# A mixture-of-experts encoder on one core: summed rows and the ninth weight unit later, bfloat16 one-hots, the last expert pair's weights in halves

## The reference, cut to what matters

```python
mod = (c_act @ w_mod[l] + b_mod[l])[:, None, :]
sh1, sc1, g1, sh2, sc2, g2 = jnp.split(mod, 6, axis=-1)
...
mix = jnp.concatenate([y_pool, y_gla], axis=-1) @ w_out[l]
x = x + g1 * mix
h = rms_norm(x) * (1.0 + sc2) + sh2
x = x + g2 * moe_ffn(h, w_router, b_router, w1[l], w3[l], w2[l])
...
# in moe_ffn, for a token t of expert e with its weight wt:
hid = jax.nn.silu(x_pad[tok] @ w1[e]) * (x_pad[tok] @ w3[e])
out[tok] += (hid @ w2[e]) * wt
...
return rms_norm(x) * final_g
```

## Time and profile before

| | us |
|---|---|
| median of 3 runs (755.04 to 759.0) | 756.38 |
| the profiled execution | 761.83 |
| its span in the trace | 760.0 |

### The profile page before, as it was taken

One profiled execution on the slowest core, in us unless ns is written; L12 is line 12 of the kernel. 1 busy time (PEld: TensorE's weight loads), 2 busy tenths in 40 slices (PEclk: granted clock), 3 DMA queues, 4 the chain that ended last, 5 costly groups with the idle time before them and its releaser, 6 DMA issues.

```text
span 760.0 us, 9258 instructions
## 1 busy us (share of the span) xinstructions
PE 700.8 (92%) x3822; PEld 388.3 (51%) x3822; DVE 343.1 (45%) x624; ACT 174.9 (23%) x309; POOL 55.5 (7%) x55
## 2 busy tenths in 40 slices
PE   3799999999898799989779999999999999998893
PEld 2578778777687444443424443443443443453442
DVE  3554988698865213323314233333333333332326
ACT  4332376532232020210110101110110110110104
POOL 2007700100000100000000000000000000000000
PEclk9899999999999899999987999999999999999997
DMA  9995353844738389998996999999999999999962
GB/s 337 388 382 202 139 200 132 314 147 206 292 137 347 131 354 427 426 425 326 430 425 281 420 415 427 426 426 426 426 428 427 426 427 428 425 428 427 429 286 110
DMA packets 38922, 259.42 MB, mean 341 GB/s; under 512 B 4126, under 2 KB 4510, under 8 KB 26208
## 3 DMA queue, kind: packets, MB, share of 16 engines
q1 hardware_dynamic: 34416, 250.11, 80.5%
q0 software_dynamic: 2688, 4.88, 1.7%
q10 hardware_dynamic: 1776, 3.84, 1.3%
HBM read 259.20 MB, written 4.19 MB: 347 GB/s over the span
## 4 chain that ended last, share of the span: by engine, by line
PE 75%; DMA 16%; DVE 7%; issue 1%; ACT 1%; SPq 1%; DVEq 0%; POOLq 0%
PE bank L904 26%; PE bank L611 16%; PE bank L913 12%; DMA ring<-in_w 8%; PE bank L921 4%; PE bank L922 3%; DMA ring<-in_w_in 3%; DMA xg_rows<-x_rows,keep 3%; DMA x_rows<-mid 2%; PE bank L878 2%; PE bank L893 2%; PE bank L929 1%; PE bank L896 1%; PE bank L731 1%; PE bank L886 1%
## 5 line engine op out<-in xcount | busy, mean ns | idle before, releaser
L904 PE MATMUL bank<-ring,low 128*64 128x512 f32 x944 | 229.7, 603 | 4.8 <-DMA ring<-in_w 4.0
L904 PEld LDWEIGHTS bank<-ring,low 128*64 128x64 f32 x944 | 74.4, 139 | 127.4 <-issue 127.4
L1678 DVE TENSOR_TENSOR x<-x,bank 128x512 f32<-128x512 f32 x136 | 84.4, 683 | 78.5 <-PE bank L922 76.7
L913 PE MATMUL bank<-ring,low 128*64 128x512 f32 x432 | 115.0, 600 | 0.9 <-DVE x L1678 0.9
L913 PEld LDWEIGHTS bank<-ring,low 128*64 128x64 f32 x432 | 35.6, 138 | 67.5 <-issue 65.9
L1668 DVE SCALAR_TENSOR_TENSOR y_raw<-bank,keep,g2b 128x512 f32<-128x512 f32 x32 | 24.0, 751 | 89.2 <-PE bank L913 89.2
L1735 DVE TENSOR_TENSOR low<-low,bank 128x512 f32<-128x512 f32 x16 | 11.0, 688 | 112.9 <-PE bank L904 112.9
L921 PE MATMUL bank<-y_hi,slot_tok 128*128 128x512 f32 x128 | 53.7, 420 | 0.2 <-DVE y_lo L1673 0.2
L922 PE MATMUL bank<-y_lo,slot_tok 128*128 128x512 f32 x128 | 50.6, 395 | 0.0
L1311 ACT COPY low<-bank 128x512 f32<-128x512 f32 x16 | 9.4, 586 | 173.6 <-PE bank L886 173.6
L1835 POOL DMA_INDIRECT xg_rows<-x_rows,keep x17 | 16.9, 996 | 432.5 <-PE bank L878 400.6
(11 more groups left out here) (248 smaller groups left out, 926.0 us busy)
## 6 DMA issues: line engine op xcount, KB each, us to landing
ring<-in_w SPq DMA_DIRECT2D x88, 2048.0 KB, 18.9
ring<-in_w_mod SPq DMA_DIRECT2D x11, 2048.0 KB, 12.3
mid<-in_w SPq DMA_DIRECT2D x11, 2048.0 KB, 17.9
ring<-in_w_in SPq DMA_DIRECT2D x4, 2048.0 KB, 21.7
ring<-in_w_out SPq DMA_DIRECT2D x2, 2048.0 KB, 10.2
x<-in_x SPq DMA_DIRECT2D x4, 512.0 KB, 6.1
mid<-in_w_mod SPq DMA_DIRECT2D x1, 2048.0 KB, 21.7
x_rows<-mid ACTq DMA_DIRECT2D x4, 512.0 KB, 13.7
```

The source lines that it names most:

```text
L904: last = mm(bk[e * CAP:(e + 1) * CAP, :], xb[:, k, e * CAP:(e + 1) * CAP], unit(n % SLOTS, KD)[:, k, :], start=k == 0, stop=k == KD - 1)
L913: last = mm(bk[e * CAP:(e + 1) * CAP, :], hid_t[:, k, e * CAP:(e + 1) * CAP], unit(n % SLOTS, KF)[:, k, hf * 512:(hf + 1) * 512], start=k ...
L1678: return v.tensor_tensor(acc[:, t, c], acc[:, t, c], bk[:, :], ALU.add)
```

## The change

- `summed_rows(10)` and `(11)` move behind `second_half(1)` on PE; on DVE the last three `mod_steps` move behind the four first residuals, and `mod_row(10)`, `(11)` behind `normed(1)`.
- Unit 8 also waits for the first gather (`gath`).
- One-hots are bfloat16. Token weights are split into three bfloat16 parts (`w_parts`), row numbers into two, so the 8 matmuls have five columns instead of two; the transposes use a bfloat16 identity, and DVE adds up the parts.
- The last pair's w3 and w2 (units 95 to 98) are loaded in halves that alternate between the two experts; the products wait for each half.
- The last pair's sums use G0 and G1 instead of Y0 and Y1, and its w2 product does not wait for DVE's adds.

```diff
-        + [f"wo0{t}" for t in range(NT)] + ["mb10", "mb11", "wo10", "wo11", "wo12", "hT00", "hT01", "wo13"]
+        + [f"wo0{t}" for t in range(NT)] + ["wo10", "wo11", "mb10", "mb11", "wo12", "hT00", "hT01", "wo13"]
...
-        onehot_t = place("onehot", LOW, [P, NT, P], F32R)
+        onehot = place("onehot", LOW, [P, NT, P], BF16)
+        ident_b = place("ident_b", LOW + 256, [P, P], BF16)
...
+        LAST_HALVES = range(len(UNITS) - 4, len(UNITS))
...
-            def expert_unit(n):
+            def expert_unit(n, half=None):
...
+                r = slice(0, kk) if half is None else slice(half * kk // 2, (half + 1) * kk // 2)
+                first = half == 0 and n in LAST_HALVES
+                sp.dma_start(unit(slot, kk)[:, r, :], w[:, e, r, :]).then_inc(first_half[n - LAST_HALVES[0]] if first else landed[slot], 16)
...
                     sp.wait_ge(h2_saved, 16 * NT)
+                    sp.wait_ge(gath, 16)
                 expert_unit(n)
...
+            for n in (LAST_HALVES[0], LAST_HALVES[2]):
+                slot_used_up(n - SLOTS)
+                slot_used_up(n + 1 - SLOTS)
+                for half in range(2):
+                    for e in range(2):
+                        expert_unit(n + e, half)
...
             second_half(0)
             second_half(1)
+            summed_rows(10)
+            summed_rows(11)
             second_half(2)
...
-                        mm(A1[e * CAP:(e + 1) * CAP, 0:2], onehot[:, t, e * CAP:(e + 1) * CAP],
+                        mm(A1[e * CAP:(e + 1) * CAP, 0:5], onehot[:, t, e * CAP:(e + 1) * CAP],
                            pair_cols[:, t, e, :], start=t == 0, stop=t == NT - 1)
                 for t in range(NT):
-                    last = nc.tensor.transpose(CA[:, t * P:(t + 1) * P], onehot[:, t, :], ident)
+                    last = nc.tensor.transpose(slots_bank[:, t * P:(t + 1) * P], onehot[:, t, :], ident_b[:, :])
...
+                    if n0 + 2 * w in LAST_HALVES and k % (KD // 2) == 0:
+                        half_landed(n0 + 2 * w, k // (KD // 2))
...
+            def last_down(n0):
+                for half in range(2):
+                    half_landed(n0 + 4, half)
+                    for hf in range(2):
+                        for k in range(half * KF // 2, (half + 1) * KF // 2):
...
+                        if half == 1:
+                            last.then_inc(y_done, 1)
...
-                if before:
+                if before and to_come > 0:
                     pe.wait_ge(acc_done, 8 * p)
...
+            for i in range(3):
+                link(v.tensor_copy(w_parts[:, :, 0:E_N, i], weights))
+                if i < 2:
+                    link(v.tensor_tensor(weights, weights, w_parts[:, :, 0:E_N, i], ALU.subtract))
...
-                v.tensor_copy(w_slot[:, buf:buf + 1], A1[:, 0:1])
-                return v.tensor_scalar(row_of[:, buf:buf + 1], A1[:, 1:2], float(S), None, ALU.add)
+                v.tensor_reduce(w_slot[:, buf:buf + 1], A1[:, 0:3], AX_X, ALU.add)
+                return v.tensor_scalar(row_of[:, buf:buf + 1], A1[:, 3:4], A1[:, 4:5], float(S), ALU.add, ALU.add)
```

More of the change, by code:

```diff
@@ L160 @@
               + [f"mb{i}" for i in range(4, 10)] + [f"rb{h}" for h in range(HEADS)]
-              + [f"wo0{t}" for t in range(NT)] + ["mb10", "mb11"] + [f"wo1{t}" for t in range(NT)] + ["rk", "cnt"])
+              + [f"wo0{t}" for t in range(NT)] + ["wo10", "wo11", "mb10", "mb11", "wo12", "wo13", "rk", "cnt"])
 assert sorted(OUT_SCALAR + OUT_VECTOR) == sorted(JOBS)
@@ L196, in build @@
         big = place("big", BIG, [P, UNIT])
-        keep = place("keep", YA + 3 * D, [P, 965])
+        keep = place("keep", YA + 3 * D, [P, 976])
         h_hi = place("h_hi", BIG, [P, KD, S], F32R)
@@ L237, in take, with place_kept @@
             at[0] += n
-            assert at[0] <= 965
+            assert at[0] <= 976
             return keep[:, at[0] - n:at[0]]
+        def place_kept(name, shape):
+            return place(name, YA + 3 * D + (at[0] + 7) // 8 * 8, shape, BF16)
         cp = take(CP_N)
@@ L366, in build @@
             "fin_table tail_in fin_ssq fin_std fin_rec fin stored")
+        first_half = [sem(f"first_half{i}") for i in range(4)]
         block = ctx.enter_context(nc.Block())
@@ L512, in extra_units @@
                     sp.dma_start(unit(n % SLOTS, kk), src).then_inc(x_weights, 16)
-            for n in range(SLOTS, len(UNITS)):
+            for n in range(SLOTS, LAST_HALVES[0]):
                 slot_used_up(n - SLOTS)
@@ L892, in slots_to_partitions, with half_landed @@
                     for t in range(NT):
-                        mm(A1[e * CAP:(e + 1) * CAP, 0:2], onehot[:, t, e * CAP:(e + 1) * CAP],
+                        mm(A1[e * CAP:(e + 1) * CAP, 0:5], onehot[:, t, e * CAP:(e + 1) * CAP],
                            pair_cols[:, t, e, :], start=t == 0, stop=t == NT - 1)
                 for t in range(NT):
-                    last = nc.tensor.transpose(CA[:, t * P:(t + 1) * P], onehot[:, t, :], ident)
+                    last = nc.tensor.transpose(slots_bank[:, t * P:(t + 1) * P], onehot[:, t, :], ident_b[:, :])
                 return last
+            def half_landed(n, half):
+                for e in range(2):
+                    if half == 0:
+                        pe.wait_ge(first_half[n + e - LAST_HALVES[0]], 16)
+                    else:
+                        pe.wait_ge(landed[(n + e) % SLOTS], landed_at(n + e))
             def up_product(n0, xb, w):
@@ L916, in down_half @@
                 return last
+            def last_down(n0):
[3 more added lines that the diff above has]
+                        for k in range(half * KF // 2, (half + 1) * KF // 2):
+                            for e in range(2):
+                                last = mm((Y0, Y1)[hf][e * CAP:(e + 1) * CAP, :], hid_t[:, k, e * CAP:(e + 1) * CAP],
+                                          unit((n0 + 4 + e) % SLOTS, KF)[:, k, hf * 512:(hf + 1) * 512],
+                                          start=k == 0, stop=k == KF - 1)
+                        if half == 1:
+                            last.then_inc(y_done, 1)
             def combine_group(g, buf, hi, lo, bk):
@@ L977, in weights @@
                 def weights(k):
+                    if k > 0 and to_come == 0:
+                        return
                     for e in range(2):
@@ L1301, in extra_begin @@
                 act.wait_ge(x_slots, j + 1)
-                nc.scalar.copy(extra_slots[:, :], CA[:, :]).then_inc(x_pt, 1)
+                nc.scalar.copy(extra_slots[:, :], slots_bank).then_inc(x_pt, 1)
             def pair(p):
@@ L1573, in _ @@
             normed(1)
+            mod_row(10)
+            mod_row(11)
             residual(1, 2)
```

47 lines of the change are left out of this document (28 added, 19 removed).

## The result

The changed kernel takes 747.08 us (median of four executions, 746.91 to 747.74) against 755.75 for the kernel before in the same comparison (four, 755.04 to 759.0): ratio 0.988, 95% interval 0.985 to 0.991. In a later comparison on one chip it took 746.7 (six, 743.9 to 749.1) against 757.6 (eleven), ratio 0.986, interval 0.980 to 0.992. Three slow executions are left out of the ratios: one of the kernel before (764.84, beside e9 to e12) and one of six each in e6 (1783.15) and e7 (2459.36), whose medians are of five. The forecast was 740.2, its own range 735 to 745, and the wider range, which takes in two rivals, 735 to 748. So the sign and the wider range held and the forecast's own range did not; the gain is 8.7 us in the first comparison, not 16.2.

A forecast was written before the change was run, and what follows sets the result against it. PE's chain was taken to bound the kernel up to 414.55 us, weight loads until 736.4, then a tail. Terms summed to -16.2 us: 761.83 to 745.6, less 5.45 gives 740.2; own range 735 to 745, wider 735 to 748.

The forecast's parts named there:

- Summed rows: Second half of w_out: its matmuls start at 193.42 without waiting for the summed rows; phase ends at 218.2, -5.1 us.
- Ninth unit: First gather: with the ninth unit held behind it, it takes 3.3 to 4 us and the row turn starts earlier, -3.1 us.
- the filler itself runs cold: Routing: weak bound of the clock term, +2 us if added DVE steps leave PE idle long enough.
- Clock: First row turn and first 64 matmuls: the filler runs into the turn, so both are warm, -2.7 us.
- bfloat16 one-hots: One-hot calls on PE's chain up to 414.55 us: five calls, each 0.9 us shorter, -4.5 us.
- Last pair: Tail: w3 starts on first halves, w2 no longer waits for DVE's adds; last adds start 0.8 us earlier.
- The median lies 5.45 below the profiled one: Whole kernel: 5.45 us subtracted from the profiled-execution forecast of 745.6, giving a median of 740.2 us.
- term 3: First row turn and first 64 matmuls: both run warm because the filler runs into the turn, -2.7 us.
- the bfloat16 turns that gain nothing: Rival on the one-hot calls: bfloat16 saves nothing on PE's chain, result 744.7 us; chance 0.10.
- the gather that is slow by itself: Rival at the first gather: its 8.40 us are its own, PE goes cold as before, result 746.0 us; chance 0.10.

The follow-up runs named there:

- e9: The changed kernel itself, run again beside executions of the kernel before on one chip: 746.7 us.
- e12: The kernel before, unchanged, profiled a third time: that execution took 753.84 us.
- e6: The changed kernel with 17 unread transposes added ahead of the last pair's w1 product: 747.9 us.
- e7: The changed kernel with 40, 12 and 26 unread transposes added in the three waits of the extra block: 748.4 us.
- e1: The changed kernel with summed rows 10 and 11 put back ahead of the second half on TensorE and VectorE: 751.9 us.
- e3: The changed kernel with float32 one-hots and two columns, as before: 750.5 us.
- e4: The changed kernel with whole units for the last pair's w3 and w2 and the old sum banks: 747.3 us.
- e8: The kernel before with 78 unread transposes added in the extra block: 757.5 us against 761.8, ratio 0.997.
- e10: The changed kernel with 78 unread transposes in the extra block and without the loop for further extra blocks: 743.0 us, ratio 0.979.
- e2: The changed kernel without SP's wait for the first gather, so the ninth unit is issued beside the gather again: 751.6 us.

## Why the prediction was right, and where it was wrong

**Summed rows, -5.1.** Right: 223.27 to 218.22 is 5.05, and e1 gives back 4.8.

**Ninth unit, -3.1.** Right in kind, a little short: the turn starts at 248.29, not 247.9, because the unread transposes took 5.89; against 251.0 that is 2.7. The gather took 4.6 us (3.3 to 4 forecast) and had landed at 247.7, before they ended. The added steps on VectorE did move the one-hots, by 1.6 us (237.47 to 239.07), and TensorE waited 1.55 for the first. The forecast's bound "the filler itself runs cold" came true: 0.69 and 0.89 of the clock from 240 to 248. That the added steps made it is not shown, since the kernel before, which has none, had it too in two of its three profiles (5.95 and 6.97 us for the 42). It cost half a microsecond and not 2, because the clock was back for the product.

**Clock, -2.7.** Right against the profiled execution: 1.97 + 15.84 became 1.04 + 13.95, 2.8 less. But the step's size belongs to that execution. In e12 the kernel before has 13.95 already.

**bfloat16 one-hots, -4.5.** Right: later calls take 0.23 + 0.33 = 0.56 us instead of 1.41, five times 0.85 = 4.3; the later calls gain nothing at the end, as the loads are the bound. e3 gives back 3.4, which includes 1.6 of VectorE's splits the other way. The Trainium skill ("TensorE: Matmul & The Clock Gate", Part 4: PE-mode transpose) has about 275 ns for one bfloat16 transpose; in the trace one lasts 0.22, and four take 0.33 to 0.34 because they start 0.08 apart, so it is the spacing that decides, as the forecast said.

**Last pair, -0.8.** Right where w1 runs at the higher clock: in e9 the time from w1's start (701.95) to w2's (721.28) is 19.33, 1.0 less than in the earlier trace rows, and the adds then come 0.3 later behind w2 (730.87 - 721.28 = 9.59 against 9.26): -0.7. In the first profile w1's 1.7 us at the lower clock ate it, a cost that I had not named. Medians (e4) can't tell 0.3 us. The Trainium skill ("DMA: Bandwidth & Descriptors", Anatomy of one DMA) gives about 2.0 us of fixed cost for a DMA that GpSimd issues. The halves, which SyncE issues, show none here: TensorE waits for no load ahead of w3 in e6, the eight land 2.5 us apart, the plain rate, and e4 is no faster without them.

**The step that failed.** "The median lies 5.45 below the profiled one: 740.2 us." This took the distance between a profiled execution and a median as a property of the measuring, the same for both kernels. It is a property of the kernel before. In both long profiles the first up product runs partly at the lower clock (15.84 and 15.62 us), and so do the block and the w1 behind it (8.90 and 8.87); in the short one the first up product runs at the higher clock (13.95), and so do the block's last sums and that w1 (7.02). The changed kernel's profiled execution lies only 0.66 above its median (747.74 against 747.08): of the 6.9 us between forecast and result, 4.8 are this step and 2.1 the sum. Against the long kind the sum is right within 0.5 to 2.1 us (745.6 forecast, 746.13 and 747.74 profiled). Against the short kind term 3 was already won, and the changed kernel, which starts the block 11 us earlier, ran it partly at the lower clock in both profiles and lost 4.4 us again. Had I taken the profile's own 745.6 as the forecast, it would have been 1.5 off the median. The profile of before showed the place: the lower clock in the block, and a product of 8.90 us where others take 7.09, right at the standstill that opens the region of the loads. I read it as given and not as something that comes and goes.

**Luck.** That 747.1 lies in the range is in part luck. The range reaches to 748 only because it takes in the rivals at 744.7 and 746.0, the bfloat16 turns that gain nothing and the gather that is slow by itself, and neither came true; the error that was made is not among the rivals.

## What to carry to other kernels

A profile is one execution: before its distance to the median is carried over to another kernel, look for the stretches at the lower clock and ask which of the timed runs have them. Where loads set the end, the last place at which they stand still is worth all that shortens the work ahead of it, and apart from the tail behind the last load nothing else is; keep the matrix engine busy just there. A filler that bridges a wait gains only if nothing behind it waits longer, as TensorE did behind the block in e7.

## What the runs showed of the hardware that was not expected

- Behind the extra block with added transposes TensorE stood 5.27 us (e7) and 1.18 us (e8) at a jump over the code of a loop that isn't run, next to a weight stream of about 425 GB/s, and went on 1.6 us after a packet of 16 KB on an instruction queue. Without the loop the stand was nil (e10), and without the transposes too. The Trainium skill ("Advanced Engine Details and Errata", Control Flow Timing) has some 51 ns for a branch and 108 ns with its comparison; the stand of e7 is some fifty times the latter, so those figures do not cover it.
- The clock's fall is not tied to one place: the same kernel had it in the first up product (0.50 at 256 us) in one execution and in the unread transposes ahead of it (0.66 at 252 us) in another, 1.9 us apart in the length of that product, and with the block 8 us apart at the end.
- Unread transposes slow down with the clock like any work: 42 took 4.75 us in the first profile of the kernel before and 6.97 in e12, 5.89 in the changed kernel and 6.29 in e2, so they can themselves become what the next step waits for.
- The last four units as eight halves of 1024 KB moved at 426 GB/s (690 to 700 us), 415 (to 710) and 423 (to 715), as whole units did before (424 to 429).
